# Reordering the beginning of a two-layer diffusion backbone: token columns, modulation chunks and first tiles on three in-order engines

## The chip, the core and the metric

The program runs on one core of one Trainium2 chip. Its engines are TensorE (PE, whose weight loads are listed as PEld), VectorE (DVE), ScalarE (ACT), GpSimd (POOL) and SyncE (SP), and 16 DMA engines move data between HBM and the core's memory. Each engine takes its own instructions in the order of the program; semaphores tie the engines together. The metric is device time of one execution in microseconds, the median of several runs.

## What is computed

There are 256 latent tokens `x` and 256 context tokens `ctx`, both 1024 wide, and two layers. Each layer has shifts, scales and gates that come from a vector `c` (latent tokens) and `c_ctx` (context tokens) through a large matrix. The kernel begins with this part of layer 0:

```python
def rms_norm(x, g):
    y = xf * lax.rsqrt(jnp.mean(xf * xf, axis=-1, keepdims=True) + RMS_EPS)
    return (y * g).astype(x.dtype)
def modulated_norm(x, g, shift, scale):
    return rms_norm(x, g) * (1 + scale) + shift
def half_step_ffn(x, g_pre, g_post, shift, scale, gate, w_gate, w_up, w_down):
    h = modulated_norm(x, g_pre, shift, scale)
    y = (jax.nn.silu(h @ w_gate) * (h @ w_up)) @ w_down
    return x + FFN_RES * gate * rms_norm(y, g_post)
...
    m_lat = (jax.nn.silu(c) @ w_mod[i] + b_mod[i]).reshape(b, N_MOD, 1, D_MODEL)
    m_ctx = (jax.nn.silu(c_ctx) @ w_mod[i] + b_mod[i]).reshape(N_MOD, D_MODEL)
    x = half_step_ffn(x, g[0], g[1], m_lat[:, 0], m_lat[:, 1], m_lat[:, 2], ...)
    ctx = half_step_ffn(ctx, g[0], g[1], m_ctx[0], m_ctx[1], m_ctx[2], ...)
```

So the first feed-forward can't start until the shift and the scale of both streams are known, each of them 1024 values out of a product with a 1024 x 1024 part of `w_mod`. After it come neighbourhood attention, further feed-forward blocks and a long convolution, none of which the change touches.

## The kernel before

**Two-part numbers.** Every matrix product is made of three: operands are split into a rounded "hi" part (ScalarE, a copy into a type that TensorE reads quickly) and a "lo" remainder (VectorE, raw minus hi), and TensorE adds hi x hi, hi x lo and lo x hi. Each weight block, chunk and activation tile thus passes ScalarE, then VectorE, then TensorE.

**Modulation loads.** The shift and scale of the first norm come as four loads of 1024 x 512, in the order scale half 0, shift half 0, scale half 1, shift half 1 (`AHEAD_LOADS`). A load is four chunks of 512 KB, numbered 0 to 15 over all; chunk n belongs to load n // 4. GpSimd issues all 16 at the start. For chunk n ScalarE runs `chunk_hi(n)` (L776), VectorE `chunk_lo(n)` (L1300), and TensorE in `ahead(l)` four products into `job_p` or `mean_p` (L1782, L1784). A split chunk lies in a slot of the weight ring (`CHUNK_SLOT`, four slots and one spare), so a later `chunk_hi` waits for the products of the chunk that had the slot (`ahead_used`): chunks 4 and 5 wait for chunks 0 and 1, chunk 12 for 7, chunk 15 for 12. When a load is done, ScalarE copies the row out (`row(l)`, L783), TensorE turns it into columns (`ahead_columns(l)`, L1792, eight records in the trace) and VectorE adds the bias (`ahead_out(l)`, L1040).

**Token columns.** For each stream ScalarE squares and sums the tokens (`square`, L644, L646), VectorE makes a diagonal of the reciprocal roots (`spread`, L1077, L1101), and TensorE transposes and scales in `norm_columns(q, t)` (L1689; q is 0 for the latent stream, 1 for the context, t is the half of the tokens; 16 records in the trace for each t). The latent columns are copied from `acc` to `z` by VectorE (L1314), since the context columns need `acc` after them.

**h.** `h` is made in halves of four tiles (kt 0 to 3 with loads 0 and 1, kt 4 to 7 with loads 2 and 3). `first_los(half)` does it for the latent stream (VectorE L1151 scales and shifts, ScalarE L656 rounds, VectorE L1155 subtracts), `second_los(half)` and `h_his(1, ...)` for the context, where VectorE does two tiles of a half (L1111) and ScalarE two (L663, L665).

**First tiles.** `first_tiles(stream, kts)` multiplies `h` with the first two weight units (24 products of 256 columns for four tiles; L1639 to L1641), and after it `both_turn` runs in eleven turns over the feed-forward. ScalarE runs the first SiLU (L739) when the first two units are complete; the next unit's products wait for it.

What sets the order is only how the calls stand in each engine's part of the program. SyncE issues weight units 0 and 1 when chunk 5 has landed, and units 2 to 5 when the last chunk has landed and the chunk that uses the slot is done with.

## Time and profile before

| | |
|---|---|
| median of 3 runs | 1360.07 us (1358.96 to 1360.62) |
| profiled execution, its own time | 1360.97 us |
| profiled execution, span | 1359.3 us |
| busy over the span: PE, DVE, ACT, POOL | 97%, 72%, 47%, 9% |
| products of the first full turn begin | 69.31 us into the span |

The span runs from the first to the last instruction; the execution's own time has 1.7 us around it. Busy time is no limit by itself: the part of the span where TensorE waits is what an order can win back.

### The profile page before, as it was taken

The numbers are of one execution on the slowest core, as the hardware profiler recorded it, in microseconds if no ns is written. First come the engines' busy times: TensorE is split into PE (matmuls) and PEld (weight loads), VectorE is DVE, ScalarE is ACT, GpSimd is POOL, SyncE is SP. The second block draws the span as 40 slices with busy tenths as digits, with TensorE's granted clock in tenths as the row PEclk, the third lists the DMA queues.
The fourth block names the chain that finished last, engine by engine and source line by source line (L and its number), as shares of the span: only waits on it lengthen the run. The fifth ranks groups of instructions, "written<-read, shape, count | busy, mean of one in ns | idle before, by whom it ended". The sixth has DMA issues, their size and how long they took to land.

```text
span 1359.3 us, 21562 instructions
## 1 busy us (share of the span) xinstructions
PE 1315.2 (97%) x7850; PEld 1126.4 (83%) x7850; DVE 981.8 (72%) x1448; ACT 633.2 (47%) x967; POOL 119.7 (9%) x209
## 2 busy tenths in 40 slices
PE   5799999999999999999999999999999999999997
PEld 3578777887778988789999989999877888899996
DVE  4788777788776785758888568886765686865554
ACT  6533333233376564664444464444455334644443
POOL 3000011111100521011111001100000000000000
PEclk9899999999999999999999999999999999999999
DMA  9355557767755753269888649875533436655662
GB/s 361 144 201 170 183 196 255 261 236 257 236 170 171 202 153 95 78 188 362 301 305 281 205 128 347 304 228 179 161 125 99 135 110 197 233 180 184 186 188 99
DMA packets 76361, 275.13 MB, mean 202 GB/s; under 512 B 9227, under 2 KB 9782, under 8 KB 75713
## 3 DMA queue, kind: packets, MB, share of 16 engines
q1 hardware_dynamic: 52128, 187.00, 42.0%
q0 software_dynamic: 24160, 87.12, 18.7%
q8 instruction: 51, 0.84, 0.2%
q14 instruction: 22, 0.17, 0.0%
HBM read 273.04 MB, written 1.05 MB: 202 GB/s over the span
## 4 chain that ended last, share of the span: by engine, by line
PE 86%; DVE 4%; ACT 3%; DMA 1%; issue 1%; ACTq 0%; DVEq 0%; SPq 0%
PE gu L1639 17%; PE gu L1641 17%; PE gu L1640 17%; PE acc L1700 8%; PE acc L1702 8%; PE acc L1701 8%; PE acc L1689 1%; DMA wlo<-in_wstream_dram 1%; PE acc L2097 1%; DVE z L1087 1%; PE acc L1973 1%; ACT whi L609 1%; DVE x_lat L1095 1%; DVE wlo_r L993 1%; PE acc L1984 1%
## 5 line engine op out<-in xcount | busy, mean ns | idle before, releaser
L1639 PE MATMUL gu<-h_hi,whi 128*128 128x256 f32 (+1 forms) x1744 | 536.6, 308 | 9.5 <-DVE h_lo L1118 6.5
L1640 PE MATMUL gu<-h_lo,whi 128*128 128x256 f32 (+1 forms) x1744 | 530.3, 304 | 0.0
L1641 PE MATMUL gu<-h_hi,wlo_r 128*128 128x256 f32 (+1 forms) x1744 | 530.0, 304 | 0.0
L993 DVE TENSOR_TENSOR wlo_r<-wlo,whi 128x1024 fp32r<-128x1024 f32 x350 | 421.3, 1222 | 91.0 <-ACT whi L609 89.3
L609 ACT ACTIVATE whi<-wlo 128x1024 fp32r<-128x1024 f32 x350 | 360.5, 1049 | 87.0 <-DMA wlo<-in_wstream_dram 86.6
L1639 PEld LDWEIGHTS gu<-h_hi,whi 128*128 128x128 f32 x1744 | 328.7, 188 | 39.6 <-issue 8.9
L1640 PEld LDWEIGHTS gu<-h_lo,whi 128*128 128x128 f32 x1744 | 328.8, 189 | 20.6 <-issue 2.2
L1641 PEld LDWEIGHTS gu<-h_hi,wlo_r 128*128 128x128 f32 x1744 | 329.2, 189 | 15.5
L1010 DVE SCALAR_TENSOR_TENSOR part<-wm,cvec,part 128x512 f32<-128x512 f32 x266 | 199.4, 750 | 6.7
L1700 PE MATMUL acc<-whi,act_hi 128*128 128x512 f32 x440 | 175.5, 399 | 0.6 <-DVE act_lo L1241 0.5
L1702 PE MATMUL acc<-wlo_r,act_hi 128*128 128x512 f32 x440 | 174.1, 396 | 0.0
L1701 PE MATMUL acc<-whi,act_lo 128*128 128x512 f32 x440 | 173.7, 395 | 0.0
L507 POOL DMA_DIRECT2D wm<-in_wmod_dram x128 | 67.6, 529 | 761.9 <-DVE part L1010 459.0
L689 ACT ACTIVATE gated<-gu 128x256 f32<-128x256 f32 x66 | 25.4, 385 | 171.8 <-PE gu L1641 171.8
L1700 PEld LDWEIGHTS acc<-whi,act_hi 128*128 128x128 f32 x440 | 82.6, 188 | 24.0 <-issue 2.6
L1702 PEld LDWEIGHTS acc<-wlo_r,act_hi 128*128 128x128 f32 x440 | 82.6, 188 | 19.9
L1701 PEld LDWEIGHTS acc<-whi,act_lo 128*128 128x128 f32 x440 | 82.7, 188 | 17.7
L1183 DVE TENSOR_TENSOR act<-gated,gu 128x256 f32<-128x256 f32 x66 | 27.8, 421 | 86.0 <-ACT gated L689 86.0
L686 ACT ACTIVATE total_hi<-part 128x512 fp32r<-128x512 f32 x38 | 24.0, 631 | 78.6 <-DVE part L1010 78.6
L743 ACT ACTIVATE act_hi<-act 128x256 fp32r<-128x256 f32 x22 | 9.2, 419 | 102.2 <-DVE act L1273 102.2
L1188 DVE TENSOR_TENSOR act_lo<-act,act_hi 128x256 fp32r<-128x256 f32 x88 | 37.2, 423 | 20.4 <-ACT act_hi L693 16.4
L693 ACT ACTIVATE act_hi<-act 128x256 fp32r<-128x256 f32 x66 | 27.6, 418 | 38.0 <-DVE act L1183 38.0
(333 smaller groups left out, 1175.9 us busy)
## 6 DMA issues: line engine op xcount, KB each, us to landing
wlo<-in_wstream_dram SPq DMA_DIRECT2D x350, 512.0 KB, 3.6
wm<-in_wmod_dram POOLq DMA_DIRECT2D x132, 512.0 KB, 5.8
area<-in_wmod_dram POOLq DMA_DIRECT2D x11, 512.0 KB, 19.8
z<-in_gate_rows_dram POOLq DMA_DIRECT2D x6, 512.0 KB, 7.3
gate_keep<-in_gate_rows_dram POOLq DMA_DIRECT2D x5, 512.0 KB, 6.0
area<-in_rpb_dram POOLq DMA_DIRECT2D x32, 64.0 KB, 3.6
x_lat<-in_x_in_dram SPq DMA_DIRECT2D x1, 1024.0 KB, 7.7
area<-in_ctx_in_dram SPq DMA_DIRECT2D x1, 1024.0 KB, 8.8
```

Source lines behind the costliest of these rows:

```text
L507: pool.dma_start(wm[:, 2 * part_:2 * part_ + 2, :], src[:, 2 * part_:2 * part_ + 2, :]).then_inc(wm_landed[part_ // 2], 16)
L609: nc.scalar.activation(whi[:, phase % RING, :], raw[:, phase % RING, :], ACT.Copy).then_inc(hi_done, 1)
L993: nc.vector.tensor_tensor(wlo[:, u.base % RING, :], raw[:, u.base % RING, :], whi[:, u.base % RING, :].bitcast(F32), ALU.subtract).then_in ...
L1010: ins = nc.vector.scalar_tensor_tensor(out=part[:, :], in0=wm[:, kt, :], scalar=c, in1=part[:, :], op0=ALU.mult, op1=ALU.add)
L1183: nc.vector.tensor_tensor(dst, gated[:, s, :], gu[:, s, T:2 * T], ALU.mult).then_inc(act_mul, 1)
L1188: nc.vector.tensor_tensor(act_lo[:, s, :], act[:, s, :], act_hi[:, s, :].bitcast(F32), ALU.subtract).then_inc(act_lo_done, 1)
L1639: nc.tensor.matmul(out_, w_hi, x_hi, start=start, stop=False, skip_group_check=True)
L1640: nc.tensor.matmul(out_, w_hi, x_lo, start=False, stop=False, skip_group_check=True)
L1641: return nc.tensor.matmul(out_, w_lo, x_hi, start=False, stop=stop, skip_group_check=True)
L1700: nc.tensor.matmul(y, x_hi[:, tok], whi[:, s, cols], start=kt_first, stop=False, skip_group_check=True)
L1701: nc.tensor.matmul(y, x_lo[:, tok], whi[:, s, cols], start=False, stop=False, skip_group_check=True)
L1702: ins = nc.tensor.matmul(y, x_hi[:, tok], wlo[:, s, cols], start=False, stop=kt_last, skip_group_check=True)
```

## The change

Only the order of calls changes, and who makes two of the context's tiles. On TensorE the latent columns (`norm_columns(0, ...)`) stand behind chunk 0 instead of chunk 3; the columns of load 0 behind load 1, and those of load 1 between the halves of the context's token columns; the first block (chunk 12) of the last load stands ahead of the latent's first products. On ScalarE and VectorE the chunks stand ahead of the row copies, of the splits of weight units 0 and 1, and of the halves of `h`. The first four context tiles are made by ScalarE alone. The split of weight unit 3 is last in the stretch.

```diff
 def scaled(q, kt):
     if q < 2:
-        return 6 * (kt // 4) + 4 * q + kt % 4 + 1
-    return 8 + 4 * (NTH[q] - 1) + kt // 4 * 2 + kt % 2 + 1
+        return 8 * q + (kt if q == 0 else kt % 4) + 1
+    return 10 + 4 * (NTH[q] - 2) + kt // 4 * 2 + kt % 2 + 1
+def on_vector(q, kt):
+    return q == 0 or kt // 2 % 2 == 0 and not (q == 1 and kt < 4)
...
-                    if q == 0 or kt // 2 % 2 == 0:
+                    if on_vector(q, kt):
...
             for n in range(1, 6):
                 chunk_hi(n)
-            row(0)
             square(1, 0)
             square(1, 1)
-            for n in range(6, 10):
+            for n in (6, 7):
+                chunk_hi(n)
+            row(0)
+            for n in (8, 9, 10):
                 chunk_hi(n)
             row(1)
+            for n in (11, 12):
+                chunk_hi(n)
+            h_his(0, range(4))
             for u in range(2):
                 split_hi(u, u)
-            h_his(0, range(4))
-            for n in range(10, 14):
-                chunk_hi(n)
             row(2)
-            for n in range(14, 16):
+            for n in (13, 14, 15):
                 chunk_hi(n)
             h_his(1, HI_ORDER[:4])
             row(3)
-            for u in (2, 3):
-                split_hi(u, u)
+            split_hi(2, 2)
             h_his(0, range(4, KT))
             h_his(1, HI_ORDER[4:])
+            split_hi(3, 3)
             load_table(ACT.Silu)
...
             def second_los(half):
-                for kt in (4 * half, 4 * half + 1):
-                    scale_columns(1, kt)
+                if half:
+                    scale_columns(1, 4)
+                    scale_columns(1, 5)
                 for kt in range(4 * half, 4 * half + 4):
                     h_lo_of(1, kt)
...
-            for n in range(1, 5):
+            for n in range(1, 4):
                 chunk_lo(n)
             for b in range(4):
                 v.wait_ge(hp_done, b + 1)
...
+            chunk_lo(4)
             chunk_lo(5)
             spread(1, 0)
             spread(1, 1)
+            for n in (6, 7, 8, 9):
+                chunk_lo(n)
             ahead_out(0)
-            for n in range(6, 10):
-                chunk_lo(n)
+            chunk_lo(10)
             ahead_out(1)
-            for u in range(2):
-                split(Unit(u))
             first_coef(0, 0)
             first_coef(1, 0)
             first_los(0)
-            for n in range(10, 14):
-                chunk_lo(n)
+            chunk_lo(11)
+            for u in range(2):
+                split(Unit(u))
+            chunk_lo(12)
+            chunk_lo(13)
             ahead_out(2)
             first_coef(0, 1)
             first_coef(1, 1)
-            for n in range(14, 16):
-                chunk_lo(n)
+            chunk_lo(14)
+            chunk_lo(15)
             second_los(0)
-            split(Unit(2))
             ahead_out(3)
             first_los(1)
+            split(Unit(2))
+            second_los(1)
             split(Unit(3))
-            second_los(1)
...
-            def ahead(l):
+            def ahead(l, kts=range(KT)):
...
-            ahead(0)
+            ahead(0, (0, 1))
             norm_columns(0, 0)
             norm_columns(0, 1)
+            ahead(0, range(2, KT))
+            ahead(1)
             pe.wait_ge(picked, 1)
             ahead_columns(0)
-            ahead(1)
             norm_columns(1, 0)
+            ahead_columns(1)
             norm_columns(1, 1)
-            ahead_columns(1)
             ahead(2)
+            ahead_columns(2)
+            ahead(3, (0, 1))
             first_tiles(LAT, range(0, 4))
-            ahead_columns(2)
-            ahead(3)
+            ahead(3, range(2, KT))
             first_tiles(CTX, range(0, 2))
             ahead_columns(3)
             first_tiles(CTX, range(2, 4))
```

The rows below are the instructions as the two programs have them; a line's number is higher by 5 to 11 in the changed file.

On TensorE, around the latent token columns (the row with `x_lat`), before: they stand behind the last products of load 0, and the columns of load 0 (`pick`) follow, then load 1 (`mean_p`).

```order
L1782 MATMUL job_p<-whi,c_both 4x512
L1784 MATMUL job_p<-wlo_r,c_both 2x512
L1689 MATMUL acc<-diag,x_lat 128x128 x16
L1792 MATMUL job_p<-pick,row_sb 128x2 x4
L1782 MATMUL mean_p<-whi,c_both 4x512
L1784 MATMUL mean_p<-wlo_r,c_both 2x512
```

And in the changed program, where only two rows like the first two stand ahead of this piece (the other half of chunk 0):

```order
L1793 MATMUL job_p<-whi,c_both 4x512
L1795 MATMUL job_p<-wlo_r,c_both 2x512
L1700 MATMUL acc<-diag,x_lat 128x128 x16
L1793 MATMUL job_p<-whi,c_both 4x512
L1795 MATMUL job_p<-wlo_r,c_both 2x512
```

The 16 column products moved ahead of chunks 1 to 3.

On ScalarE, from chunk 1 to the roundings of the first half of `h`, before (`row_sb` is a row copy, L644 and L646 the context's squares, `whi<-wlo` the weight units):

```order
L776 ACTIVATE whi<-wm 128x1024 x3
L776 ACTIVATE whi<-area 128x1024 x2
L783 ACTIVATE row_sb<-job_p 4x512
L644 ACTIVATE gu,ssum<-area 128x1024
L646 ACTIVATE root<-ssum,eps 128x1
L644 ACTIVATE gu,ssum<-area 128x1024
L646 ACTIVATE root<-ssum,eps 128x1
L776 ACTIVATE whi<-area 128x1024 x4
L783 ACTIVATE row_sb<-mean_p 4x512
L609 ACTIVATE whi<-wlo 128x1024 x2
L656 ACTIVATE h_hi<-z 128x256 x4
L776 ACTIVATE spare_hi<-area 128x1024
```

And in the changed program, from the second of the context's roots on:

```order
L651 ACTIVATE root<-ssum,eps 128x1
L781 ACTIVATE whi<-area 128x1024 x2
L788 ACTIVATE row_sb<-job_p 4x512
L781 ACTIVATE whi<-area 128x1024 x2
L781 ACTIVATE spare_hi<-area 128x1024
L788 ACTIVATE row_sb<-mean_p 4x512
L781 ACTIVATE whi<-area 128x1024 x2
L661 ACTIVATE h_hi<-z 128x256 x4
L614 ACTIVATE whi<-wlo 128x1024 x2
L788 ACTIVATE row_sb<-job_p 4x512
L781 ACTIVATE spare_hi<-area 128x1024
```

Chunks 10 to 12 moved ahead of the roundings, the weight units behind them, and the row copy of load 2 ahead of chunk 13.

On VectorE, from the bias of load 0 to the first half of `h`, before:

```order
L1040 TENSOR_TENSOR mod<-job_p,bm 128x8
L1300 TENSOR_TENSOR wlo_r<-area,whi 128x1024 x4
L1040 TENSOR_TENSOR mod<-mean_p,bm 128x8
L993 TENSOR_TENSOR wlo_r<-wlo,whi 128x1024 x2
L1070 SCALAR_TENSOR_TENSOR coef<-mod,sm 128x4 x2
L1151 TENSOR_SCALAR z<-z,coef,mod 128x256 x2
```

And in the changed program, from the bias of load 1 on:

```order
L1047 TENSOR_TENSOR mod<-mean_p,bm 128x8
L1077 SCALAR_TENSOR_TENSOR coef<-mod,sm 128x4 x2
L1158 TENSOR_SCALAR z<-z,coef,mod 128x256 x2
L1162 TENSOR_TENSOR h_lo<-z,h_hi 128x256
L1158 TENSOR_SCALAR z<-z,coef,mod 128x256
L1162 TENSOR_TENSOR h_lo<-z,h_hi 128x256
L1158 TENSOR_SCALAR z<-z,coef,mod 128x256
L1162 TENSOR_TENSOR h_lo<-z,h_hi 128x256 x2
L1308 TENSOR_TENSOR wlo_r<-area,whi 128x1024
L1000 TENSOR_TENSOR wlo_r<-wlo,whi 128x1024 x2
```

The two weight units moved from ahead of the first half of `h` to behind it and chunk 11.

## Rows read from the trace of the kernel before

**Rows 1.** The page's head and its first part: busy time, share, instructions.

```profile
span 1359.3 us, 21562 instructions
...
PE 1315.2 (97%) x7850; PEld 1126.4 (83%) x7850; DVE 981.8 (72%) x1448; ACT 633.2 (47%) x967; POOL 119.7 (9%) x209
```

**Rows 2.** Waits of TensorE from 69.3 us to the end: total, times, longest.

```profile
PE gu L1639 <- DVE h_lo L1118: 5.0, 5, 1.2
```

**Rows 3.** Windows, TensorE alone: window, length, busy (records), granted clock, DMA share, GB/s.

```profile
38.00:43.40 5.40, 0.00 (x0) 0.82 0.58 212
43.40:48.30 4.90, 4.85 (x15) 0.50 0.00 0
...
69.30:110.00 40.70, 40.69 (x175) 1.00 0.53 179
```

**Rows 4.** Timeline of TensorE: start, us, what, records [idle before, releaser].

```profile
15.88 0.59 PE L1782 MATMUL job_p<-whi,c_both 128*4 128x512 f32 x1 [3.46 <-DVE wlo_r L1300]
...
20.53 0.61 PE L1784 MATMUL job_p<-wlo_r,c_both 128*2 128x512 f32 x1
20.95 3.76 PE L1689 MATMUL acc<-diag,x_lat 128*128 128x128 f32 x32
24.64 1.05 PE L1792 MATMUL job_p<-pick,row_sb 4*128 4x2 f32 x8
25.62 0.40 PE L1782 MATMUL mean_p<-whi,c_both 128*4 128x512 f32 x1
25.86 0.40 PE L1784 MATMUL mean_p<-wlo_r,c_both 128*2 128x512 f32 x1
...
65.78 0.39 PE L1639 MATMUL gu<-h_hi,whi 128*128 128x256 f32 x1 [1.29 <-DVE h_lo L1118]
...
83.85 0.40 PE L1700 MATMUL acc<-whi,act_hi 128*128 128x512 f32 x1
```

**Rows 5.** Timeline of ScalarE, the same columns.

```profile
17.86 1.06 ACT L776 ACTIVATE whi<-area 128x1024 fp32r<-128x1024 f32 x1 [0.45 <-DMA area<-in_wmod_dram]
...
21.67 1.00 ACT L644 ACTIVATE gu<-area 128x1024 f32<-128x1024 f32 x1
...
24.41 1.99 ACT L776 ACTIVATE whi<-area 128x1024 fp32r<-128x1024 f32 x2
...
66.08 0.56 ACT L665 ACTIVATE h_hi<-acc,mod,coef 128x256 fp32r<-128x256 f32 x1
66.65 1.28 ACT L621 ACT_TABLE_LOAD   x1
...
68.56 0.60 ACT L739 ACTIVATE gated<-gu 128x512 f32<-128x512 f32 x1 [0.42 <-PE gu L1641]
```

**Rows 6.** Timeline of VectorE, the same columns.

```profile
12.49 0.29 DVE L1101 TENSOR_SCALAR diag<-ident,rstd 128x128 f32<-128x128 f32 x1
...
14.60 3.50 DVE L1300 TENSOR_TENSOR wlo_r<-wm,whi 128x1024 fp32r<-128x1024 f32 x3 [0.46 <-ACT whi L776]
...
23.41 2.48 DVE L1314 COPY z<-acc 128x512 f32<-128x512 f32 x4 [4.18 <-PE acc L1689]
...
27.81 4.62 DVE L1300 TENSOR_TENSOR wlo_r<-area,whi 128x1024 fp32r<-128x1024 f32 x4
...
38.44 0.74 DVE L1151 TENSOR_SCALAR z<-z,coef,mod 128x256 f32<-128x256 f32 x2
...
41.23 0.42 DVE L1155 TENSOR_TENSOR h_lo<-z,h_hi 128x256 fp32r<-128x256 f32 x1
...
59.76 0.16 DVE L1040 TENSOR_TENSOR mod<-mean_p,bm 128x8 f32<-128x8 f32 x1
60.01 0.74 DVE L1151 TENSOR_SCALAR z<-z,coef,mod 128x256 f32<-128x256 f32 x2
...
82.28 0.43 DVE L1188 TENSOR_TENSOR act_lo<-act,act_hi 128x256 fp32r<-128x256 f32 x1 [0.15 <-ACT act_hi L743]
```

**Rows 7.** DMA issue of chunk 10 (issued at 6.75 us): size, us to landing.

```profile
area<-in_wmod_dram POOLq DMA_DIRECT2D x1, 512.0 KB, 21.0
```

More of the change, by code:

```diff
@@ L1777, in ahead @@
                     pe.wait_ge(mod_ready, l - 1)
-                for kt in range(KT):
+                for kt in kts:
                     n, cols = 4 * l + kt // 2, slice(kt % 2 * 512, kt % 2 * 512 + 512)
```

## The prediction, made before the changed kernel ran

> **What bounds the kernel now.** I read the busy shares first: TensorE is busy 97% of the 1359.3 us span [rows 1]. Then TensorE's waits from 69.3 us on: the largest of all totals 5.0 us, in five pieces [rows 2], and the first turns run with 40.69 us busy in 40.70 [rows 3]. From the first full turn on the kernel is bound by TensorE's own work, and each wait left there is on ScalarE or VectorE work that moves along with it; nothing is tied to an absolute time. So what the change does to the start of the first turn (69.31 us) goes one to one into the end. The windows show how loose the beginning is: from 38.0 to 43.4 us TensorE does nothing at all, and when it comes back its granted clock is 0.50, the 1.2 GHz level, until 48.3 [rows 3]. That hole is VectorE's and ScalarE's: chunks 10 to 13 stand behind the first half of `h` in both, and that half behind two weight units. Chunk 10 had landed at 6.75 + 21.0 = 27.75 us [rows 7].
>
> **Prices, from rows.** A chunk costs ScalarE 0.95 us in a row of them, 1.04 alone (two in 1.99) [rows 5]; VectorE 1.13 (four in 4.62 against three in 3.50) [rows 6]; and TensorE starts on it 1.28 after VectorE did (14.60 to 15.88) [rows 4, 6]; VectorE starts 1.09 after ScalarE when it waits. Four products of a chunk take 0.94 at the full level (25.62, 25.86) and 1.70 at half (12 products from 15.88 to 20.95) [rows 4]. All 32 records of one stream's columns take 3.69 at the full level, 0.115 each; a load's columns 0.98 [rows 4].
>
> **The change, step by step.** Up to 12.78 us nothing differs: the latent diagonal is made at 12.49 [rows 6], chunk 0's products are over.
>
> 1. *Latent columns at 12.85 instead of 20.95.* No row shows such columns at the half level. Bounds: 0.115 a record (no effect) and 0.213, half the pace of a 512-column product's 0.427 (they would take as many cycles as 256 columns each, if 0.115 is TensorE's own time). I take 0.213, since the chunk products just before and after are at half pace. The level rose twice in the trace after about five gapless microseconds of products, from 15.88 to 20.95 and from 43.4 to 48.3 [rows 3, 4]; I count 4.9 from 12.85, so it rises at 17.75: 23 records at 0.213, nine at 0.115, end at 18.8. Chunks 1 to 3 follow at 0.94 each, end at 21.6.
> 2. *The cost of that.* Chunk 5 needs chunk 1's slot. Before it started at 17.86, as it landed [rows 5]; now chunk 1's products end at 19.9, so chunk 5 starts at 19.9, two later. The context's squares, 2.74 us from 21.67 to 24.41 [rows 5], follow at 20.9 because the row copy no longer stands ahead, and chunks 6 and 7 start at 23.6 and 24.6. VectorE has copied the columns (2.48) [rows 6] by 20.5 and done chunks 4 and 5 by 22.7; both diagonals of the context stand ahead of chunk 6, and the second root comes at 23.8, so chunk 6 starts at 24.7, chunk 7 at 25.9. TensorE does chunk 7 from 27.1 to 28.1.
> 3. *Columns of loads 0 and 1.* 28.1 + 0.98 + half of the context's token columns 1.85 + 0.98 = 31.9; the row copy of load 1 (behind chunk 10, at 29.2) is ready for it. VectorE adds the bias at 32.0 and begins `h` at 32.25, the same quarter microsecond as 59.76 to 60.01 [rows 6]. Before that was 38.44 [rows 6], with two weight units (2.3) in between.
> 4. *VectorE leads.* The half of `h` takes 3.2 (38.44 to 41.65) [rows 6], then chunk 11 and two units: 32.25 + 3.2 + 3 x 1.13 = 38.8, chunk 12, on TensorE at 40.1. Chunk 13 and later fit behind: chunk 15 waits for chunk 12's slot (41.2), and its lo is done for TensorE at 43.8.
> 5. *TensorE leads.* From 40.1 without a gap: chunk 12 0.94, 24 latent products 2.8 (65.78 to 68.56) [rows 4, 5], chunks 13 to 15 2.8, 12 context products 1.4, columns of load 3 0.98: 49.1. ScalarE makes all four context tiles itself, 0.92 each, from 42.2 to 45.9: done before TensorE asks for the first (46.7), and its two extra tiles cost nothing. Without that cover each would cost 0.9. The last bias is added at 49.2, `h` begins at 49.45 instead of 60.01: **10.56 us**.
> 6. *Behind it the order is the same*, 8.55 us from 60.01 to the first SiLU at 68.56, except that unit 3's split now stands between the last rounding (66.08, so 55.5) and the table load: rounding 0.46, split 1.05, table 1.28, a 0.2 us filler. ScalarE is free at 58.55, TensorE's products end at 58.0: 0.55 lost. The first turn starts at 59.25: **10.0 us early**.
> 7. *VectorE enters the first turn 1.1 us later against TensorE*, by unit 3's split. The tightest place is the second lo of the activations, done at 82.28 + 0.43 = 82.71 where TensorE takes it at 83.85 [rows 4, 6]: a margin of 1.14. I take nothing here; the other end is 0.3.
>
> Weight units 2 and 3 are issued once the last chunk has landed, chunk 8 and 9 being done; units 4 and 5 behind chunks 14 and 15: all come earlier, and DMA, 0.53 busy in the first turns [rows 3], has the room. The sum against the profiled execution: 1360.97 - 10.0 = 1351.0; that run is 0.9 over the median, so for the median 1350.1. I say 1350.3, with a little for step 7.
>
> **The rivals.**
>
> *The clock rises late.* At 20.95 as before, whatever runs. Then the columns stay slow to 19.7, chunk 1 ends at 21.6, chunk 5 starts 1.7 later than in step 2, and this goes through to the end: gain 8.4, time 1351.7. The Trainium skill, page "TensorE: Matmul & The Clock Gate", section "Part 1: The HAM clock gate", says that "the default state is throttled, and activity releases the throttle", and that the moment differs from run to run. By that rule the later moment is as possible as mine; the trace's two rises agree with the first half of it and leave the second open.
>
> *The columns don't pay for the half level, or it ends sooner.* Chunk 0's products, just ahead, start the count as well. The columns end by 17.1, chunk 5 starts at 18.2, and from then on landings hold (chunk 10 at 27.75): gain 11.2, time 1348.9.
>
> *The clock falls in a new gap.* Between chunk 5 (done at 23.8) and chunk 6 (26.0) TensorE has nothing for 2.2 us. The gap of 5.4 us and more before 43.4 cost the level [rows 3]; the one of 1.29 us before 65.78 did not [rows 4]. If this one does, the chunk, both columns and the context's token columns of steps 2 and 3 run at half pace for some five microseconds: about 3 us later, gain 7, time 1353.
>
> *Slower: the half level stays.* If TensorE kept the half level from 12.85 to the first turn, each product on the path would cost double: chunks 1 to 3 2.8, chunk 7 and the columns of step 3 4.8, step 5 9.0, the last products 2.8: 19.4 more against 10.0 won, 1369.5. It decides from about 10 us of such work on, that is if the level is still down at the latent's first products. Against it: both stretches of gapless work in the trace raised it.
>
> *No change.* The early microseconds would have to be lost in the turns. Only VectorE's 1.1 us can be: one split, once; even lost whole and twice it leaves 8. That leaves an error in my chain of waits, for instance a row copy that blocks a chunk for longer than I see.
>
> **How the numbers follow.** Chances: as forecast (gain 9 to 10.8) 0.42; sooner 0.2; late clock 0.17; fall in the gap or a mixture of small losses (gain 3 to 7.7) 0.15; no change 0.03; slower 0.03. The likeliest case's own range is 1349.3 to 1351.1. For eight in ten I take 1348.2 to 1355.0, which leaves out the largest losses. A measurement of this kernel can tell about 0.2%, 2.7 us, from no change, so faster is 0.94.
>
> **What would show it.** Right: latent columns start near 12.85 on TensorE; chunk 5's rounding near 19.9; VectorE's first scaling of `h` near 32.3; no hole between 38 and 43; half pace nowhere after 18; the last half of `h` near 49.5; the first turn's product near 59.3; TensorE gapless behind it. The later stages keep their lengths. Wrong: half pace past 21 us, a hole of over a microsecond behind 30 us, or a TensorE wait on the activations' lo in the first turn.

## The result and the profile after

The changed kernel takes 1352.05 us (median of 10 runs, 1349.95 to 1355.7), the kernel before in the same session 1359.89 (10 runs, 1358.96 to 1361.43): ratio 0.9943, 95% interval 0.9935 to 0.9952. It is 7.8 us faster; the forecast was 9.8, a median of 1350.3. The profiled execution took 1352.54 us, its span is 1350.9. That is 8.4 shorter than before; the forecast was 10.0.

The page of the changed kernel, its head and the busy times (answers to [rows 1]):

```profile
span 1350.9 us, 21563 instructions
## 1 busy us (share of the span) xinstructions
PE 1314.2 (97%) x7850; PEld 1127.7 (83%) x7850; DVE 980.5 (73%) x1446; ACT 633.8 (47%) x969; POOL 118.0 (9%) x209
```

TensorE has the same 7850 products as before. Its busy time is 1.0 us less, and its idle time is 7.4 us less (span less busy: 36.7 in place of 44.1). Its windows in the changed kernel; columns are stretch, length, busy (products), granted clock, DMA share, GB/s (answers to [rows 3]):

```profile
12.80:18.00 5.20, 4.99 (x30) 1.00 1.05 413
14.00:16.00 2.00, 2.00 (x12) 1.00 1.05 412
16.60:18.20 1.60, 1.60 (x16) 1.00 0.99 407
37.60:40.20 2.60, 1.31 (x10) 1.00 1.03 411
40.20:43.70 3.50, 3.50 (x16) 0.53 0.23 89
43.70:50.00 6.30, 6.30 (x43) 0.99 0.65 210
60.57:101.27 40.70, 40.60 (x173) 1.00 0.54 175
```

The hole of 5.4 us is gone. There is a row that the forecast did not have: from 40.2 to 43.7 the granted clock is 0.53, the 1.2 GHz level, behind a stretch in which TensorE was busy for 1.31 of 2.60 us, most of it with the tiny products of the columns. Sixteen products fit into those 3.5 us; in a trace below without the fall it is 28, though not all of the same size. The first three rows are a warning to the reader: the granted clock reads 1.00 in all of them, although the columns run at half pace until about 16.5. The 2.00 us from 14.00 hold 12 of the column records, the 1.60 us from 16.60 hold 16. From the start of one record to the next it is 0.213 us before 16.5 and 0.112 after it (worked out from the single records of the trace). Early in a trace it is the pace of like products that tells the level.

TensorE's timeline, changed kernel (answers to [rows 4]); columns as there:

```profile
13.01 5.48 PE L1700 MATMUL acc<-diag,x_lat 128*128 128x128 f32 x32 [0.39 <-DVE diag L1108]
18.25 0.47 PE L1793 MATMUL job_p<-whi,c_both 128*4 128x512 f32 x1
...
25.57 0.40 PE L1793 MATMUL mean_p<-whi,c_both 128*4 128x512 f32 x1 [1.48 <-DVE wlo_r L1308]
...
27.72 1.05 PE L1803 MATMUL job_p<-pick,row_sb 4*128 4x2 f32 x8
...
38.21 1.05 PE L1803 MATMUL job_p<-pick,row_sb 4*128 4x2 f32 x8 [0.68 <-ACT row_sb L788]
39.94 0.39 PE L1793 MATMUL mean_p<-whi,c_both 128*4 128x512 f32 x1 [0.68 <-DVE wlo_r L1308]
...
40.39 0.62 PE L1793 MATMUL mean_p<-whi,c_both 128*4 128x512 f32 x1
...
56.63 0.39 PE L1650 MATMUL gu<-h_hi,whi 128*128 128x256 f32 x1 [1.29 <-DVE h_lo L1125]
...
60.57 0.48 PE L1650 MATMUL gu<-h_hi,whi 128*128 128x512 f32 x1 [0.83 <-ACT gated L744]
```

The columns begin close to the forecast place (13.01, forecast 12.85) and take 5.2 us to the next product (forecast 6.0). Two waits of 0.68, ahead of 38.21 and of 39.94, stand around one us of columns, and from 40.39 on a chunk product takes 0.62 in place of 0.39. The first full turn begins at 60.57, which is 8.74 earlier than the 69.31 of before.

ScalarE and VectorE, changed kernel (answers to [rows 5, 6]):

```profile
19.51 1.06 ACT L781 ACTIVATE whi<-area 128x1024 fp32r<-128x1024 f32 x1 [1.92 <-PE job_p L1795]
...
27.95 1.06 ACT L781 ACTIVATE spare_hi<-area 128x1024 fp32r<-128x1024 f32 x1 [0.38 <-DMA area<-in_wmod_dram]
...
59.85 0.58 ACT L744 ACTIVATE gated<-gu 128x512 f32<-128x512 f32 x1
```

```profile
31.77 0.17 DVE L1047 TENSOR_TENSOR mod<-mean_p,bm 128x8 f32<-128x8 f32 x1 [1.50 <-PE mean_p L1803]
...
32.04 0.73 DVE L1158 TENSOR_SCALAR z<-z,coef,mod 128x256 f32<-128x256 f32 x2
...
50.60 0.17 DVE L1047 TENSOR_TENSOR mod<-mean_p,bm 128x8 f32<-128x8 f32 x1 [3.90 <-PE mean_p L1803]
50.86 0.73 DVE L1158 TENSOR_SCALAR z<-z,coef,mod 128x256 f32<-128x256 f32 x2
```

Chunk 5 waits 1.92 for chunk 1's products and starts at 19.51; `h` begins at 32.04, its last half at 50.86. VectorE's 3.90 us of idle time ahead of that half says who leads there: TensorE.

Behind the first turn little differs. The weight loads' waits in the changed kernel (PEld; us in total, times, longest), from 60 to 110 us, have one that is new, for the lo part of the activations:

```profile
PEld acc L1711 <- DVE act_lo L1196: 0.3, 1, 0.3
```

### The profile page after: what moved, and what is told of

It reads as the page before. It is cut to its first block, busy times and chain, and to the rows that moved or that the text cites. A ratio compares the mean times of both kernels' runs of the same rounds, so it can differ in the third digit from the quotient of the medians.

```text
span 1350.9 us, 21563 instructions
## 1 busy us (share of the span) xinstructions
PE 1314.2 (97%) x7850; PEld 1127.7 (83%) x7850; DVE 980.5 (73%) x1446; ACT 633.8 (47%) x969; POOL 118.0 (9%) x209
## 4 chain that ended last, share of the span: by engine, by line
PE 89%; DVE 4%; ACT 4%; DMA 1%; issue 1%; SPq 0%; ACTq 0%; DVEq 0%
PE gu L1650 18%; PE gu L1652 17%; PE gu L1651 17%; PE acc L1711 8%; PE acc L1713 8%; PE acc L1712 8%; PE acc L1700 2%; PE acc L2110 1%; DVE z L1094 1%; ACT whi L614 1%; PE acc L1986 1%; DVE x_lat L1102 1%; DMA wlo<-in_wstream_dram 1%; PE acc L1997 1%; DMA x_lat<-in_x_in_dram 1%
## 5 line engine op out<-in xcount | busy, mean ns | idle before, releaser
L1713 PEld LDWEIGHTS acc<-wlo_r,act_hi 128*128 128x128 f32 x440 | 82.6, 188 | 19.9
```

The source lines that it names most:

```text
L1713: ins = nc.tensor.matmul(y, x_hi[:, tok], wlo[:, s, cols], start=False, stop=kt_last, skip_group_check=True)
```

## The experiments

All twelve were run in turns with the kernel before, in three sessions in which before had medians of 1360.04, 1360.08 and 1359.66 us. Each has five runs, but experiment 5 eleven and experiment 8 six. Each trace is of one of these runs. This table is worked out from their results and traces. `h` is when VectorE begins the latent's first half, then come the times from there to the last half, from there to the first full turn, and from there to the end of the span; "columns" is the length of the 32 latent column products.

| kernel | median (lowest to highest) | ratio to before, 95% | columns | h | to last half | to turn | rest |
|---|---|---|---|---|---|---|---|
| before | 1360.0 | | 3.76 | 38.44 | 21.57 | 9.30 | 1290.0 |
| changed | 1352.05 (1349.95 to 1355.7) | 0.9935 to 0.9952 | 5.48 | 32.04 | 18.82 | 9.71 | 1290.3 |
| 1 middle filled | 1351.6 (1349.7 to 1352.16) | 0.9918 to 0.9945 | 6.13 | 32.52 | 17.31 | 9.72 | 1290.4 |
| 2 columns back | 1354.98 (1354.1 to 1356.26) | 0.995 to 0.9977 | 3.74 | 34.44 | 18.83 | 9.71 | 1290.2 |
| 3 splits early | 1349.36 (1348.44 to 1350.96) | 0.991 to 0.9937 | 4.52 | 31.04 | 17.50 | 8.74 | 1289.5 |
| 4 start filled | 1351.42 (1350.92 to 1353.91) | 0.9928 to 0.9955 | 3.84 | 31.93 | 17.42 | 9.71 | 1290.6 |
| 5 columns alone | 1358.51 (1357.4 to 1360.03) | 0.9981 to 0.9998 | 5.53 | 36.16 | 22.10 | 9.29 | 1289.6 |
| 6 all filled, splits early | 1350.47 (1349.61 to 1351.36) | 0.9918 to 0.9944 | 3.84 | 31.72 | 17.65 | 8.76 | 1290.4 |
| 7 middle filled, splits early | 1349.14 (1348.46 to 1352.78) | 0.9916 to 0.9942 | 5.53 | 31.81 | 17.51 | 8.74 | 1289.3 |
| 8 VectorE's tiles | 1351.79 (1349.88 to 1355.69) | 0.9931 to 0.9955 | 5.29 | 31.84 | 18.83 | 9.71 | 1290.2 |
| 9 latent first | 1351.82 (1350.67 to 1352.17) | 0.9925 to 0.9952 | 6.54 | 33.07 | 17.82 | 9.71 | 1289.9 |
| 10 units first | 1351.6 (1350.54 to 1352.3) | 0.9925 to 0.9953 | 4.37 | 33.01 | 16.56 | 9.71 | 1289.6 |
| 11 units first, splits early | 1350.57 (1350.56 to 1353.1) | 0.9923 to 0.995 | 5.47 | 33.03 | 17.53 | 8.75 | 1289.6 |
| 12 latent first, splits early | 1353.46 (1351.83 to 1355.88) | 0.9942 to 0.997 | 5.08 | 31.70 | 19.71 | 8.75 | 1289.9 |

How to read it: behind the change "to turn" has two values only, 9.71 or 9.72 with the split of unit 3 last, 8.74 to 8.76 with both splits early. The order of the splits decides it. "columns", "h" and "to last half" also differ between traces of kernels with the same order in that place: by the clock, and for "h" also by the moment at which chunk 10 lands (experiments 4 and 6). The forecast had 32.25, 17.2 and 9.8.

### 1: the middle filled

```diff
+            filler(gu[:, 1, 0:P], 3)
             ahead_columns(2)
+            filler(gu[:, 1, 0:P], 3)
             ahead(3, (0, 1))
```

`filler(bank, n)` multiplies the identity with itself n times into a bank that is overwritten later.

> The changed kernel with three small products of the identity (0.23 us each at the full level) put on TensorE ahead of the columns of load 2 and three behind them, where TensorE waited 0.68 and 0.68 us in the trace. Theory: in the changed kernel TensorE ran at half level from 40.2 to 43.7 us because it had next to nothing to do from 37.5 to 39.9; the 3.5 us at half pace cost 1.7, and the filler takes that away: first turn's product near 58.9 instead of 60.57, no half pace behind 20 us, median near 1350.3. Rival: the level falls there whatever TensorE does in those two microseconds, then the half pace stays and the median is that of the changed kernel, 1352.0. A second rival: the filler is in the way of the columns, 0.1 to 0.3 us slower.

1351.6. TensorE's timeline of this kernel:

```profile
37.84 0.83 PE L1821 MATMUL gu<-ident 128*128 128x128 f32 x6
38.68 1.05 PE L1803 MATMUL job_p<-pick,row_sb 4*128 4x2 f32 x8
39.66 0.94 PE L1821 MATMUL gu<-ident 128*128 128x128 f32 x6
40.41 0.41 PE L1793 MATMUL mean_p<-whi,c_both 128*4 128x512 f32 x1
```

In this trace the level does not fall: "to last half" is 17.31 where the changed kernel had 18.82. But the medians differ by 0.45 only, inside both intervals, and traces 3, 4, 9 and 10 have no fall there either, without this filler. So they do not show that the filler is what kept the level. The run decides nothing on the filler. It does show what the fall costs between these two traces, 1.5 us.

### 2: the latent columns back behind chunk 3

```diff
-            ahead(0, (0, 1))
+            ahead(0)
             norm_columns(0, 0)
             norm_columns(0, 1)
-            ahead(0, range(2, KT))
```

VectorE's chunk 4 stands ahead of the copy of the columns again.

> The changed kernel with the latent token columns back behind all four chunks of load 0 on TensorE, and their copies back behind chunk 4 on VectorE; everything else of the change stays. Theory: the columns end at 24.6 again, the copies at 25.8, so chunk 5's lo is made at 25.8 instead of 21.7 and chunk 7's products end near 31.1 instead of 27.6: 3.4 us of the gain hang on this part, median 1355.4. Rival: VectorE's first half of h and the units behind it set the pace whatever comes before, then the median stays at 1352. Other rival: with the columns at the full level and chunk 5 at its landing (17.9 instead of 19.5), the part was worth less than nothing, 1351 or under.

1354.98: 2.9 us slower than the changed kernel by medians. The two intervals of the ratio overlap by 0.0002 at their ends (0.9950 and 0.9952), and the traces agree with the medians: the first turn begins at 62.98 in place of 60.57, 2.4 later, with the same fall of the clock in both. TensorE's timeline of this kernel:

```profile
19.95 3.74 PE L1699 MATMUL acc<-diag,x_lat 128*128 128x128 f32 x32
...
30.12 1.05 PE L1802 MATMUL job_p<-pick,row_sb 4*128 4x2 f32 x8
```

The columns now run at the full level, in 3.74 in place of 5.48, and that costs time: they stand in the way of the load's chunks. The columns of load 0 come at 30.12 (27.72 in the changed kernel) and `h` 2.40 later. Everything behind has the lengths of the changed kernel, 18.83 and 9.71.

### 3: both splits early

```diff
             h_his(1, HI_ORDER[:4])
+            for u in (2, 3):
+                split_hi(u, u)
             row(3)
-            split_hi(2, 2)
             h_his(0, range(4, KT))
             h_his(1, HI_ORDER[4:])
-            split_hi(3, 3)
             load_table(ACT.Silu)
```

And the same on VectorE, both ahead of the bias of load 3.

> The changed kernel with the splits of weight units 2 and 3 ahead of the row copy and the bias of load 3, in holes of 2.0 us on ScalarE (46.2 to 48.2) and 3.9 us on VectorE (46.7 to 50.6). Theory: two things go away, ScalarE's split of unit 3 ahead of the table load (the SiLU then starts when the products end, 0.4 us sooner) and VectorE's split of unit 2 between the two streams' last halves (1.13 us on the path): median 1350.4, first turn near 59.0, TensorE's wait of 1.29 us ahead of the context's last tiles down to 0.2. Rival: only the SiLU's part is real, because ScalarE's own tile behind the latent's last one ends last: 1351.6. Rival on the other side: the splits push the row copy and the bias of load 3, 1352.5.

1349.36, 2.7 under the changed kernel and faster than expected. TensorE in this kernel, windows and then timeline:

```profile
40.20:43.70 3.50, 3.50 (x28) 1.00 0.15 59
```

```profile
37.22 1.05 PE L1803 MATMUL job_p<-pick,row_sb 4*128 4x2 f32 x8 [0.68 <-ACT row_sb L788]
38.94 0.39 PE L1793 MATMUL mean_p<-whi,c_both 128*4 128x512 f32 x1 [0.67 <-DVE wlo_r L1308]
53.76 0.39 PE L1650 MATMUL gu<-h_hi,whi 128*128 128x256 f32 x1 [0.74 <-DVE h_lo L1125]
57.28 0.47 PE L1650 MATMUL gu<-h_hi,whi 128*128 128x512 f32 x1 [0.42 <-ACT gated L744]
```

Two things are in it. The order is worth 0.96 behind the last half: the waits for the last `h_lo` and for the SiLU are 0.74 and 0.42 where the changed kernel has 1.29 and 0.83, and "to turn" repeats in experiments 6, 7, 11 and 12. Some 0.2 of it is paid ahead of the last half, as the rival had it, because the splits hold up the row copy of load 3: from chunk 12's first product to the columns of load 3 it is 8.25 us here and 8.05 in experiment 4, both without a fall and without a filler there. The other 2.3 us by which the first turn is earlier in this one trace are the clock: columns 0.96 shorter, and no fall at 40 although the two waits of 0.68 are there as they were (0.68 and 0.67). The moved splits can't have done that, since they lie behind it.

### 4: the start filled

```diff
+            pe.wait_ge(ident_landed, 16)
+            filler(acc[:, 3, 0:P], 20)
             pe.wait_ge(c_lo, 1)
             ahead(0, (0, 1))
```

> The changed kernel with 20 small products of the identity on TensorE before its first chunk, when it has nothing to do (from about 3.6 to 10.7 us). Theory: the latent columns took 5.24 us at half level instead of 3.69, and chunk 5, which waits for chunk 1's products, started at 19.5 instead of at its landing, 17.9. With the level up beforehand the columns end near 16.8, chunk 5 starts at 17.9, chunk 7 ends near 26.0; then the landing of chunk 10 (27.9) and the row copy behind it hold, so 1.1 us gained: median 1350.9. Rival: the columns take their 5.2 us whatever the clock, then nothing changes, 1352.0. Other rival: the late part of the beginning meets another moment of the clock, then first turn and median move by up to 1.7 either way.

1351.42. TensorE's timeline of this kernel, then a window of it:

```profile
12.78 3.84 PE L1700 MATMUL acc<-diag,x_lat 128*128 128x128 f32 x32 [1.25 <-DVE diag L1108]
...
21.63 0.59 PE L1793 MATMUL mean_p<-whi,c_both 128*4 128x512 f32 x1 [2.23 <-DVE wlo_r L1308]
22.02 0.63 PE L1795 MATMUL mean_p<-wlo_r,c_both 128*2 128x512 f32 x1
```

```profile
21.30:28.00 6.70, 6.37 (x25) 0.75 1.03 409
```

And ScalarE's timeline of this kernel:

```profile
28.99 1.06 ACT L781 ACTIVATE spare_hi<-area 128x1024 fp32r<-128x1024 f32 x1 [1.02 <-DMA area<-in_wmod_dram]
```

The columns run at full level, 1.6 us shorter, and TensorE is through with load 0 sooner. Then it waits 2.23 us for chunk 4's lo, and behind that wait a product takes 0.63. This is the mechanism of the forecast's third rival, a fall in a new gap, one gap ahead of where it looked. But `h` begins at 31.93, so next to nothing is left of the 1.6, and the fall is not what holds it: experiment 6, without any fall, has `h` at 31.72. What holds it is chunk 10, as this experiment's expectation had it: ScalarE waits 1.02 us for its landing and starts on it at 28.99 (27.95 in the changed kernel), and the row copy, the columns of load 1 and the bias stand behind it.

### 5: the columns alone

The kernel before, with only the TensorE edit of experiment 2 the other way round.

> The kernel before, with one part of the change alone: the 32 latent column products stand behind chunk 0 on TensorE instead of behind chunk 3. The orders of VectorE and ScalarE are those of before. If what the products of the beginning wait for is TensorE's own order, taking 3.7 us of columns out of the row between chunks 3 and 7 brings the columns of load 0 forward by about 2, the hole of 38 to 43 us moves forward with them, and the kernel gains 2.0: 1358.0. Rival: chunk 5 on ScalarE now starts two later, since chunk 1's slot comes free later, both weight units and the first half of h still stand ahead of chunks 10 to 13, and the place of the columns is worth nothing by itself: 1360.0. In that case the gain of the whole change needs the re-ordering of VectorE and ScalarE to be had at all.

1358.51, ratio 0.9989: 1.6 faster than before, with an interval that ends just short of no change, and less than the 0.2% that the prediction took as the least that can be told. In the trace the first turn begins at 67.55, 1.76 early. The hole is still there, as long as before (5.66 us, before 5.64), and it has only moved forward, from 43.45 to 41.17 at its end; TensorE's timeline and window of this kernel:

```profile
41.17 0.59 PE L1782 MATMUL job_p<-spare_hi,c_both 128*4 128x512 f32 x1 [5.66 <-DVE spare_lo L1300]
```

```profile
40.20:45.50 5.30, 4.33 (x13) 0.51 0.13 50
```

So the place of the columns is worth 1.6 by itself and 2.9 inside the whole. All the other parts of the change together are worth about 5 (1360.0 to 1354.98). No run has the order of the chunks on VectorE and ScalarE alone. That it is the main part of the 5 rests on the traces: the hole of 5.6 us, behind a wait for VectorE's chunk 10, is there without it and gone with it.

### 6: every gap filled, splits early

```diff
             ahead(0, range(2, KT))
-            ahead(1)
+            pe.wait_ge(xt_copied, 1)
+            filler(acc[:, 0, 0:P], 6)
+            ahead(1, range(0, 4))
+            filler(acc[:, 0, 0:P], 5)
+            ahead(1, range(4, KT))
```

Together with the edits of experiments 1, 3 and 4.

> The changed kernel with the splits of units 2 and 3 early, as in the third experiment, and filler products of the identity in every gap of TensorE that was seen to cost the clock: 20 ahead of chunk 0, 6 behind load 0, 5 between chunks 5 and 6, and 6 around the columns of load 2. The fillers' results are overwritten. If the clock's falls in the gaps are what the changed kernel lost against the forecast, no stretch behind 13 us shows half pace, the last half of h starts near 48.3 us, and the median is 1348.3, with a spread under 2 us. Rival: the fillers stand in the way of products that were ready (each 0.06 to 0.2 us, 37 in all) and the level moves by its own phase all the same: 1349.4 or above, no better than the splits alone.

1350.47: the first half of the expectation holds, the second doesn't. The level is up throughout (window of this kernel):

```profile
12.90:50.00 37.10, 35.56 (x234) 1.00 0.91 348
```

All five runs lie within 1.75 us, the narrowest band of the kernels with early splits. But `h` begins at 31.72, 0.7 later than in experiment 3. ScalarE's timeline of this kernel says what it waits for:

```profile
26.87 1.06 ACT L781 ACTIVATE whi<-area 128x1024 fp32r<-128x1024 f32 x1 [1.35 <-DMA area<-in_wmod_dram]
28.77 1.06 ACT L781 ACTIVATE spare_hi<-area 128x1024 fp32r<-128x1024 f32 x1 [0.84 <-DMA area<-in_wmod_dram]
```

The landings of chunks 9 and 10 hold it now; in the changed kernel ScalarE waited 0.38 for chunk 10 and no more. Faster products ahead of a landing only wait longer for it. The landings are later here, too: in experiment 3 ScalarE waited for the same two and started on them at 25.83 and 27.58, 1.0 and 1.2 earlier. The other kernel with a late chunk 10 is experiment 4, which also has the filler at the start; whether that filler is the reason is open. And "rest" has a single wait of 1.0 us for an activation's lo, between 1000 and 1200 us, that experiments 3 and 7 lack (experiment 4 has one of 0.9). A full level all the way is no better than the splits alone.

### 7: the middle filled, splits early

> The changed kernel with the early splits and only the 6 identity products around the columns of load 2. The splits were worth 2.7 by medians, the middle filler 0.45. If the half pace from 40.2 us on is a matter of the emptiness before it, the two add up to 1349.0, and the slowest runs, 3 above the median in the changed kernel, are gone. Rival: the early splits fill nothing on TensorE but change when the gap comes, and the filler adds nothing to them: 1349.4 with the same spread as the third experiment.

1349.14, but one of the five runs took 1352.78: the spread is not gone. The median is that of experiment 3, so the filler adds nothing that can be measured.

### 8: context tiles 0 and 1 scaled by VectorE again

```diff
-                    if on_vector(q, kt):
+                    if q == 0 or kt // 2 % 2 == 0:
...
-                if half:
-                    scale_columns(1, 4)
-                    scale_columns(1, 5)
+                for kt in (4 * half, 4 * half + 1):
+                    scale_columns(1, kt)
```

With the old numbers in `scaled`.

> The changed kernel, but VectorE again scales context tiles 0 and 1 for ScalarE to round, as before the change, instead of ScalarE making them from the diagonal form itself. The forecast said that ScalarE's two extra tiles cost nothing, because they lie beside TensorE's chunk products. If so this is worth nothing either way: 1352.0, within 0.5. Rival: the handover of the two tiles was a cost of either side: 0.9 us a tile on the path, so 1350.2 if ScalarE's tiles were late, or 1353.0 if VectorE's are.

1351.79 against 1352.05, and "to last half" and "to turn" are 18.83 and 9.71, those of the changed kernel. The part is worth nothing that can be told.

### 9: the latent's first products ahead of chunk 12

```diff
-            ahead(3, (0, 1))
             first_tiles(LAT, range(0, 4))
-            ahead(3, range(2, KT))
+            ahead(3)
```

> The changed kernel, but TensorE takes the latent's first 24 products ahead of chunk 12 again, as before the change. In the trace of the changed kernel TensorE waits 0.68 us for chunk 12's lo at 39.94 while the latent's tiles have been ready since 35. With the tiles first that wait is filled, chunk 15's slot comes free some three microseconds later, at about 43, and ScalarE and VectorE still make chunk 15 by 44.5, when TensorE asks for it. So this part of the change by itself should be worth nothing or cost 0.7: 1351.3 here against 1352.05. Rival: chunk 15 is late by the two to three microseconds by which its slot is late, and the part was worth 1 or more: 1353.0 or above.

1351.82, the same as the changed kernel. Chunk 15 is late, as the rival had it, but by little; TensorE's timeline of this kernel:

```profile
46.71 0.40 PE L1793 MATMUL mean_p<-whi,c_both 128*4 128x512 f32 x1 [0.62 <-DVE wlo_r L1308]
```

It is 0.68 won ahead of chunk 12 and 0.62 given back ahead of chunk 15. With the level up all the way the stretch "to last half" is 17.82, against 17.31 to 17.65 of the traces with the changed order and no fall. This trace is of use for the clock as well: TensorE waited 2.44 us ahead of chunk 6, at a granted clock of 1.00, and kept the level.

```profile
26.59 0.40 PE L1793 MATMUL mean_p<-whi,c_both 128*4 128x512 f32 x1 [2.44 <-DVE wlo_r L1308]
```

### 10: units 0 and 1 ahead of h

```diff
             row(1)
+            for u in range(2):
+                split_hi(u, u)
             for n in (11, 12):
                 chunk_hi(n)
             h_his(0, range(4))
-            for u in range(2):
-                split_hi(u, u)
```

And the same on VectorE, ahead of the bias of load 1.

> The changed kernel, but ScalarE and VectorE split weight units 0 and 1 behind chunk 10, ahead of the first half of h, as before the change; chunks 11 and 12 stay ahead of h on ScalarE. If what mattered was that chunks 10 to 12 come ahead of h, the place of the units is free: in the trace of the changed kernel VectorE waits 1.5 us for the bias of load 1 at 31.8, the units fill that, h begins 0.9 later and chunk 12 is done 1.0 to 1.5 earlier. 0.5 faster: 1351.5. Rival: the 2.3 us of splits delay h and with it chunk 11, whose products TensorE then waits for, and the columns of load 2: 0.8 slower, 1352.9.

1351.6, as expected in size and not to be told from the changed kernel. `h` begins at 33.01, TensorE waits for chunk 11:

```profile
37.42 0.39 PE L1793 MATMUL job_p<-whi,c_both 128*4 128x512 f32 x1 [1.57 <-DVE wlo_r L1308]
```

and chunk 12 follows without a wait, since VectorE is done with it by then:

```profile
40.17 0.40 PE L1793 MATMUL mean_p<-whi,c_both 128*4 128x512 f32 x1
```

That is 0.23 later than in the changed kernel, so against that trace the place of the two units costs next to nothing, and `h` being 1 us later is made up for ahead of chunk 12. It is not free in every state. VectorE's two units end at 32.75 here and at 32.76 in experiment 11, whose clock rose 2.4 later, and `h` begins behind them. In experiment 3, whose clock rose as early as in this trace, `h` began at 31.04, chunk 12 at 38.94 and the last half at 48.54 (49.57 here). The last half is earlier than the changed kernel's 50.86 because this trace has no fall at 40.

### 11: units first, splits early, middle filled

> The seventh experiment (early splits of units 2 and 3, 6 identity products around the columns of load 2) with the units 0 and 1 ahead of the first half of h as well. The two places do not meet: if the units' place fills a wait, 0.5 better than the seventh's 1349.1: 1348.7, in one band of under 2 us. Rival: VectorE is the one that leads between 32 and 40 us in either order, so nothing changes: 1349.1.

1350.57, four of the runs within 0.5, one at 1353.1. There is no gain over experiment 7, whose median is 1.4 lower. The two ratios' intervals overlap, but the traces have the same sign: with the clock alike (columns 5.47 and 5.53, no fall) the first turn begins at 59.31 here and at 58.06 there. Chunk 11 is 1.2 later on TensorE (37.44 against 36.21), and the second half of the filler, which in experiment 7 stood in a wait for chunk 12, now stands in the way of products that are ready: chunk 12 begins at 40.86, in experiment 10 without the filler at 40.17.

### 12: latent first, splits early

> The third experiment (early splits of units 2 and 3) with the latent's first products ahead of chunk 12. TensorE's 0.7 us wait ahead of chunk 12 is filled with real products, so it has one gap less in the stretch in which the clock fell in the changed kernel. If gap and level are linked as the traces suggest, 0.7 and a steadier level: 1348.7. Rival: as in the ninth experiment, chunk 15 comes late and takes the 0.7 back: 1349.4 or above.

1353.46, clearly the wrong way: 4.1 slower than experiment 3. TensorE and then ScalarE, timelines of this kernel:

```profile
45.36 0.39 PE L1793 MATMUL mean_p<-whi,c_both 128*4 128x512 f32 x1 [0.62 <-DVE wlo_r L1308]
...
50.06 1.05 PE L1803 MATMUL mean_p<-pick,row_sb 4*128 4x2 f32 x8 [1.80 <-ACT row_sb L788]
```

```profile
42.99 1.06 ACT L781 ACTIVATE whi<-gate_keep 128x1024 fp32r<-128x1024 f32 x1 [3.26 <-PE mean_p L1795]
...
47.55 2.04 ACT L614 ACTIVATE whi<-wlo 128x1024 fp32r<-128x1024 f32 x2
49.44 0.57 ACT L788 ACTIVATE row_sb<-mean_p 4x512 f32<-4x512 f32 x1
```

Both edits were harmless alone. Together, ScalarE starts chunk 15 at 42.99 (41.53 in the changed kernel, whose clock had fallen by then), its four context tiles follow, and the two early splits stand ahead of the row copy, which TensorE now waits 1.80 for. Both edits had drawn on the same slack of ScalarE. "To last half" is 19.71, 2.2 over experiment 3: the two waits are 2.42 together, the wait of 0.67 ahead of chunk 12 is saved, and the rest is in small gaps of 0.1 around the context's products. The first turn is 2.9 later than in experiment 3's trace. This trace is of the fastest of the five runs, and what the slower ones have on top, 1.6 by the median, was not traced.

## Why the prediction was right, and where its sizes were off

The direction, the mechanism and the range held. The forecast's likeliest case gave 10.0 for the profiled execution and got 8.4; the missing part is one term. The likeliest case's own range, 1349.3 to 1351.1, was missed by 1 us, and the gain lies outside the band "as forecast" (9 to 10.8). That 8.4 is also the number of the first rival is chance: the clock did not rise late in this trace. Two of the prediction's own signs of being wrong did occur: half pace past 21 us, from 40.2 to 43.7, and a wait on the activations' lo in the first turn, of 0.3.

- **Step 1, columns at half level**: right. They start at 13.01, and a record at half level takes 0.213 as forecast; they pay for it, the bound "no effect" is out. The rise was forecast at 17.75 and came at about 16.5, so the columns were through at 18.25 instead of 18.8. But the moment is no property of the order: across kernels with the same order up to there and no filler the columns took from 4.37 to 6.54. So the first rival ("rises late") and the second ("ends sooner") both occur, as states of single runs. Experiment 9's trace comes near the first: the rise is at about 18.7, the columns end at 19.28 (the rival had 19.7), `h` begins at 33.07. Experiment 3's has the second: chunk 5 starts at 18.20 (the rival had 18.2), then landings hold, `h` begins at 31.04. The prediction had treated them as alternatives of which one is true.
- **Steps 2 and 3**: chunk 5 at 19.51 (19.9), columns of load 0 at 27.72 (28.1), `h` at 32.04 (32.25). Right within 0.4, with the rise 1.3 earlier than forecast. Experiment 2 put the columns back and cost 2.9 us.
- **Step 4, VectorE leads; chunk 12 on TensorE at 40.1**: 39.94, behind a wait of 0.68 for VectorE's lo, so VectorE does lead in this trace. Experiment 10 shows how narrowly: with the two units elsewhere in VectorE's row chunk 12 begins at 40.17 with no wait for VectorE, and chunk 11 and the row copy and columns of load 2 set the time.
- **Step 5, TensorE without a gap to 49.1**: the step that was mis-sized. There is no gap behind 40, but the first 3.5 us run at the 1.2 GHz level, and the last half begins at 50.86 instead of 49.45. Where the level stayed, the stretch from `h` took 17.31 to 17.65 (experiments 1, 3, 4, 6 and 7; 9 to 12 have another order in it), the forecast had 17.2; with the fall it took 18.82, three times alike (the changed kernel, experiments 2 and 8). The term left out is 1.2 to 1.5 us, the difference of these; 3.5 us at half the pace would make 1.7 where nothing else waits. The forecast did name a fall in a new gap, but looked for it between chunks 5 and 6, where TensorE waited 1.48 and kept the level. It took chunk 12 at 40.1 from VectorE's row, and did not ask how little TensorE has to do in the 2.6 us before it.
- ScalarE's extra tiles at no cost: right (experiment 8).
- **Step 6, 0.55 lost at the table load**: 9.71 against 9.30 from the last half to the first turn, so 0.41. Experiment 3 shows that more was to be had: with both splits ahead of the row copy it is 8.74.
- **Step 7, margin of 1.14 on the activations' lo**: used up just so. A weight load waits 0.3 there, one product is 0.1 longer. The same wait of 0.3 is in all seven traces with the split of unit 3 last (the changed kernel, experiments 1, 2, 4, 8, 9 and 10) and in none of the five with it early (3, 6, 7, 11 and 12), nor in before. The forecast took nothing here.
- **Slower, the half level stays**: no trace. The later stages kept their lengths: 1289.3 to 1290.6 us from the first turn on in all thirteen, before 1290.0.

The sum for the profile: 10.0 forecast, less 1.4 for the fall, is 8.6; 8.74 was won at the first turn and 8.4 at the end of the span, 0.3 of step 7 in between. The medians differ by 7.8: the profiled execution of before lay 1.1 over its median, that of the changed kernel 0.5 over its own. In the changed kernel two runs in ten took 1350.0, six 1351.8 to 1352.5 and two 1355.7. The first group is the forecast's; that it is the runs without the fall at 40 is an argument from the traces' 1.2 to 1.5, since no run of that group was profiled. The two slowest have a mean granted clock of 0.994 where the others have 0.996 to 0.998; in which stretch it falls there is open, and it came in experiments 8 and 12 as well.

The Trainium skill, page "TensorE: Matmul & The Clock Gate", section "Part 1: The HAM clock gate", says that the moment of the rise differs by about 500 ns from run to run. The traces agree that it differs, and not on the size. In the changed kernel and in experiment 10 chunk 0's products began at 10.75 and the columns at 13.01 and 13.02, and the columns took 5.48 us in the one and 4.37 in the other. The rise came at about 16.5 and 14.2, and in experiment 9 (columns from 12.99) at about 18.7: 4.5 us between the last two. It shows in how many records a window holds, at full pace in experiment 10, first row, and at half pace in experiment 9, second row:

```profile
14.00:16.00 2.00, 2.00 (x20) 1.00 1.07 418
16.60:18.20 1.60, 1.60 (x9) 1.00 1.03 422
```

The best order found is experiment 3's, 1349.36 (ratio 0.9924) beside the changed kernel's 0.9943; experiment 7, the same order with a filler, has 1349.14. The traces show about 0.8 of it at the first turn (0.96 less 0.2) and the wait of 0.3 behind it. The medians' 2.7 has the clock's scatter in it, and the two intervals overlap.

## What to carry to other kernels

Where three in-order engines hand pieces on, look for the engine that leads in each stretch and bring its pieces forward; the others' pieces need only be early enough. Do not take the rest of the leading engine's row for free: the same shift of two weight units moved chunk 12 by 0.23 us against the changed kernel's trace and the first turn by 1.25 against experiment 7's. Two edits that each cost nothing may draw on the same slack, so try them together before counting both. And when work is moved on TensorE, ask of each stretch how much real work is in it: the clock fell behind one with short waits and tiny products in three traces and kept its level behind the same waits in two others, so a single trace of it is one throw, not the rule.

## What the runs showed of the hardware

- TensorE's level rose at moments that differ by 4.5 us (about 14.2 us in experiment 10, 18.7 in experiment 9) between executions whose products begin within 0.5 us of each other, and the columns' time follows (4.37 to 6.54 us for 32 records, 3.74 at full level; 0.213 from record to record at the half level, 0.112 at the full one).
- The same gap came with a fall of the level in one execution and not in the next: 0.68, columns, 0.68 ahead of chunk 12 was followed by a granted clock of 0.53 in the changed kernel (a like fall in experiments 2 and 8) and of 1.00 in experiments 3 and 4. A wait of 2.23 us was followed by products at half pace in experiment 4, and one of 2.44 ahead of chunk 6 was not in experiment 9, nor one of 1.48 in the changed kernel. The length of a wait alone does not tell.
- The full level for the latent columns gained nothing that could be told (experiments 4 and 6): the columns were 1.6 us shorter and `h` began at most 0.3 earlier, because ScalarE waited 1.02 and 0.84 us for the landing of chunk 10.
- A landing moves between executions, too: ScalarE, waiting for chunk 10, could start on it between 27.46 us (experiment 12) and 28.99 (experiment 4).
